# A two-block transformer kernel: activation buffers 384 bytes higher, every weight slot 192 bytes below the tokens modulo 512

## The reference

```
# first block: 16 meta tokens are put ahead of the 512
h = h + 0.5 * swiglu(rmsnorm(h, norm_ffn1), w_ffn1_in, w_ffn1_out)        # "f1" in the kernel
u = rmsnorm(h, norm_mix)
...  = split(u @ w_in)                       # forgetting attention, retention, two gates
mixed = g_a * (y_a @ w_o_fox) + g_b * (y_b @ w_o_ret)
h = h + mixed @ w_out
h = h + 0.5 * swiglu(rmsnorm(h, norm_ffn2), w_ffn2_in, w_ffn2_out)        # "f2"
# second block: 512 tokens and 256 context tokens, two layers
for l in range(2):
    y, yc = mixing_sublayer(...)             # three branches, then merge_groups(...) @ w_o
    x = layer_norm(ALPHA * x + g1 * y) * ln1_g[l] + ln1_b[l]
    x = layer_norm(ALPHA * x + g2 * swiglu_2(modulate(x, sh2, sc2), ...)) * ln2_g[l] + ln2_b[l]
    ...                                      # the context likewise, in layer 0 alone
```

## Time and profile before

| what | value |
|---|---|
| median of 3 runs | 3315.65 us (3312.38 to 3316.1) |
| profiled execution | 3318.37 us, its span 3316.6 us |
| PE busy | 3199.3 us, 96% of the span, 24458 multiplications |
| PEld busy | 2982.2 us, 90% |
| DVE, ACT, POOL busy | 1802.8, 1392.6, 482.1 us (54%, 42%, 15%) |
| mean busy share of the 16 DMA engines | 29.1% for SP's queue, 3.2% for POOL's |
| TensorE clock granted | 0.993 of full speed |

### The profile page before, as it was taken

How to read it: one execution, slowest core, us unless ns; L and a number is a source line. 1 busy time by engine, 2 the same in 40 slices (tenths; PEclk the granted TensorE clock), 3 DMA queues, 4 the chain that set the end, 5 groups by cost and what they waited for, 6 DMA issues and landing times. The chain is left out here.

```text
span 3316.6 us, 60366 instructions
## 1 busy us (share of the span) xinstructions
PE 3199.3 (96%) x24458; PEld 2982.2 (90%) x24458; DVE 1802.8 (54%) x3099; ACT 1392.6 (42%) x2533; POOL 482.1 (15%) x471
## 2 busy tenths in 40 slices
PE   8999999999999999999999999999999999989998
PEld 7999988787778899998889889999998789979997
DVE  4666553536634456666445773222227645776765
ACT  4222232337633332225447754212125557654444
POOL 1010020036500010010113201001010103111110
PEclk9999999999999999999999999999999999999999
DMA  4445422122123334453211331211214311435653
GB/s 161 165 163 175 153 75 79 59 71 65 52 77 96 108 123 170 170 175 126 68 31 35 122 115 52 64 61 61 64 58 126 101 56 46 139 88 140 165 144 99
DMA packets 107074, 339.68 MB, mean 102 GB/s; under 512 B 12144, under 2 KB 16496, under 8 KB 106672
## 3 DMA queue, kind: packets, MB, share of 16 engines
q1 hardware_dynamic: 97616, 311.65, 29.1%
q0 software_dynamic: 8752, 23.65, 3.2%
q10 hardware_dynamic: 432, 0.52, 0.0%
HBM read 324.38 MB, written 2.10 MB: 98 GB/s over the span
## 5 line engine op out<-in xcount | busy, mean ns | idle before, releaser
L2710 DVE TENSOR_TENSOR r_Wbasel<-r_Wf,r_Wbaseh 128x1024 fp32r<-128x1024 f32 (+3 forms) x286 | 359.1, 1257 | 504.3 <-ACT r_Wbaseh L2006 503.8
L2006 ACT ACTIVATE r_Wbaseh<-r_Wf 128x1024 fp32r<-128x1024 f32 (+3 forms) x286 | 291.2, 1022 | 418.3 <-PE PS L1325 313.8
L1323 PE MATMUL PS<-r_X1h,r_Wbaseh 128*128 128x264 f32 (+2 forms) x1216 | 392.2, 323 | 14.8 <-DVE r_X1l L3058 5.4
L1324 PE MATMUL PS<-r_X1l,r_Wbaseh 128*128 128x264 f32 (+2 forms) x1216 | 378.1, 311 | 0.0
L1325 PE MATMUL PS<-r_X1h,r_Wbasel 128*128 128x264 f32 (+2 forms) x1216 | 377.8, 311 | 0.0
L2710 DVE TENSOR_TENSOR r_Wtopl<-r_Wf,r_Wtoph 128x1024 fp32r<-128x1024 f32 (+3 forms) x147 | 174.1, 1185 | 207.1 <-ACT r_Wtoph L2006 206.7
L1323 PE MATMUL PS<-r_X2h,r_Wbaseh 128*128 128x256 f32 (+1 forms) x888 | 274.4, 309 | 5.8 <-DVE r_Wbasel L2710 2.5
L1325 PE MATMUL PS<-r_X2h,r_Wbasel 128*128 128x256 f32 (+1 forms) x888 | 266.7, 300 | 0.0
L1324 PE MATMUL PS<-r_X2l,r_Wbaseh 128*128 128x256 f32 (+1 forms) x888 | 266.5, 300 | 0.0
L1323 PEld LDWEIGHTS PS<-r_X1h,r_Wbaseh 128*128 128x128 f32 x1216 | 231.0, 190 | 38.1 <-issue 8.1
L1324 PEld LDWEIGHTS PS<-r_X1l,r_Wbaseh 128*128 128x128 f32 x1216 | 231.0, 190 | 13.7 <-issue 2.4
(11 more groups left out here) (520 smaller groups left out, 9971.4 us busy)
## 6 DMA issues: line engine op xcount, KB each, us to landing
r_Wf<-in_wmod SPq DMA_DIRECT2D x96, 512.0 KB, 3.6
r_Wf<-in_f_in SPq DMA_DIRECT2D x88, 512.0 KB, 4.4
r_Wf<-in_g_in SPq DMA_DIRECT2D x69, 512.0 KB, 3.5
r_Wf<-in_w_o SPq DMA_DIRECT2D x40, 512.0 KB, 4.4
r_Wf<-in_f_out SPq DMA_DIRECT2D x32, 448.0 KB, 4.2
r_Wf<-in_g_out SPq DMA_DIRECT2D x32, 448.0 KB, 3.4
r_SR<-in_g_in SPq DMA_DIRECT2D x38, 256.0 KB, 3.4
r_SR<-in_g_in POOLq DMA_DIRECT2D x38, 256.0 KB, 5.5
```

Source lines behind the costliest of these rows:

```text
L1323: self.e.matmul(o, wh, xh, start=first, stop=False)
L1324: self.e.matmul(o, wh, xl, start=False, stop=False)
L2006: e.activation(p.w(i, cols)[0], p.Wf[:, i % NW, 0:cols], ACT.Copy).then_inc(*p.hi.did(i))
L2710: e.tensor_tensor(l, p.Wf[:, i % NW, 0:cols], h.bitcast(F32), ALU.subtract).then_inc(*p.lo.did(i))
```

## The change

No instruction is added or removed. Two paddings move buffers, and the second feed-forward part of the first block gets token buffers of its own.

- `MB` moves from the top area to the end of the constants, and P0, the first byte of the token area, lies 256 + 128 = 384 bytes higher; all that is placed from P0 on moves along.
- The `mixed` and `latent` slots get 320 bytes of padding ahead of them, and TOP, the place of the `top` slots, is 320 lower.
- `n3` and `f2` use X5 instead of X1, and H2 takes its rows: 512 tokens instead of 528, so that 2048 bytes are the step of a feature tile. X5 lies in the bytes of X1.

```
-TOP = 188224
+TOP = 187904
...
+        self.MB, p = at("MB", [128, 2, 32], F32, p)
-        P0 = p
+        P0 = p + 128
...
-        self.H2[0], p = at("H2h", [128, 8, T1], F32R, P1)
-        self.H2[1], p = at("H2l", [128, 8, T1], F32R, p)
+        self.X5 = [None, None]
+        self.X5[0], p = at("X5h", [128, 8, TX], F32R, P0)
+        self.SQ5, _ = at("SQ5", [128, 8, TX], F32, P0)
+        self.XC5, _ = at("XC5", [128, 8, TX], F32, p)
+        self.X5[1], p = at("X5l", [128, 8, TX], F32R, p)
+        assert p <= P1
+        self.H2[0], p = at("H2h", [128, 8, TX], F32R, P1)
+        self.H2[1], p = at("H2l", [128, 8, TX], F32R, p)
...
-        p = self.weight_slots("mixed", 3, P2)
+        p = self.weight_slots("mixed", 3, P2 + 320)
...
-        self.MB, pm = at("MB", [128, 2, 32], F32, pm)
...
-        self.weight_slots("latent", 2, p)
+        self.weight_slots("latent", 2, p + 320)
...
-        n3 = add("n3", [a_, b_], lambda k, c: vec("ffn2", k), None, self.X1, 0, self.XC1, self.SQ1, self.PAm,
+        n3 = add("n3", [a_, b_], lambda k, c: vec("ffn2", k), None, self.X5, 16, self.XC5, self.SQ5, self.PAm,
...
-        f2 = Ffn("f2", self.X1, 0, [a_, b_], self.H2, self.TM2, n3, lambda m, c0: 0.5)
+        f2 = Ffn("f2", self.X5, 16, [a_, b_], self.H2, self.TM2, n3, lambda m, c0: 0.5)
```

## The result

The changed kernel takes 3292.36 us, the median of four runs (3288.65 to 3300.39), beside 3315.87 us for the kernel before (four runs, 3312.38 to 3316.1). The ratio is 0.9931, with a 95% interval from 0.9911 to 0.9952: 23.5 us faster, where 52.7 were forecast, and above the range of 3254 to 3285. The profiled execution is the fastest of the four, 3288.65 us. All lines of this program stand six higher than in the kernel before, so that the three multiplications are lines 1329 to 1331. Its trace lacks 16 records of one other line, 1838, which is why the page counts 16 multiplications fewer.

What follows compares the result with a forecast made beforehand. PE was taken as the bound, busy 3199.3 of 3316.6 us, its pace depending on operand addresses. Terms 31.9 + 15.5 + 8.5 + 1.9 - 2.1 = 55.7 us, less 3 for waits, gave a median of 3263 us; range 3254 to 3285.

Steps and rivals of the forecast that it cites:

- The argument from the earlier trace: Adjacent g0 streams of H3, same shape: 120.0 ns with `top` slots at distance 0, 113.3 with `base` at +192.
- Rival 3: No change: the poor state takes all the gain (3319 us), or addresses are not the cause (3316); chance 0.04.
- All 24 sums of that kind: `lin_tok` on X2, tokens stationary and weights moving, at -192 before the change; taken to show 113.3 ns for that distance.
- Rival 1: Distance -192 with stationary weights has two states; A, B and C run at 115.0 ns, 3284 us; chance 0.09.
- A: `top`, `latent` and `mixed` products going from distance 0 to -192: 4,764 multiplications at 6.7 ns, 31.9 us gained.
- B: X1 and H2 products in f2, from a changing distance to -192: 3,168 multiplications at 4.9 ns, 15.5 us gained.
- C: `base` products going from +192 to -192: 5,088, of which 1,923 in the poor state gain 4.4 ns each, 8.5 us.
- The exchange of weights and tokens: Inference that -192 gives 113.3 ns also with weights stationary and tokens moving, the reverse of `lin_tok` on X2.
- D: 512-wide YA and YB products with `base`, 384 at +192: 5 ns each, 1.9 us gained, at least nothing.
- E: `lin_tok` on X2 going from -192 to +192: 480 multiplications at 4.4 ns, 2.1 us lost, at best nothing.
- I took off 3 us: Allowance for PE waits growing, at H4's low part in g1 and at `top` weights, as PE gets faster.

Runs made afterwards that it cites:

- e6: Changed kernel with weight slots 16 bytes into their tiles and all slots at distance -112 modulo 256; 3342.08 us, ratio 1.0067 to the kernel before.
- e9: Distance -112 like e6, but with token tensors, not weights, moved 16 bytes into their allocations; 3286.33 us, ratio 0.991 to the kernel before.
- e1: Streams alone, not the whole kernel: 16 distances from -256 to 224 in steps of 32; -192 ended at 113.3 ns in 10 of 12 starts.
- e5: Streams alone, not the whole kernel: distances -128 to 120 in steps of 8, some starts behind distance 0; -112 ran at 113.3 ns behind all 15 starts.
- e8: Streams alone, not the whole kernel: four weight places by sixteen token places; at -112, 113.3 ns with weights at 0, 120.0 with weights at 16.
- e2: The change with stationary weights at +192 in place of -192, tokens left where they were; 3320.82 us, ratio 1.001 to the kernel before.

## Why the prediction was right in direction and wrong in size

**Right.** PE sets the time, the change works by addresses alone, and it makes the kernel faster. The argument from the earlier trace rows held: 113.3 ns stands where 120.0 stood. Rival 3's version in which addresses mean nothing is out: e6 and e9 issue the same instructions on other addresses, and lie 0.7% above and 0.9% below the kernel before. The Trainium skill ("SBUF — State Buffer", section "Who interferes with whom") has the single rule that only the port pair shared by VectorE and GpSimd causes contention. These runs do not agree with what the prediction drew from it, that the residues mean nothing, and the measurement decides.

**The step that failed** is "All 24 sums of that kind [...] settle at 113.3 [...] So I take 113.3 ns for distance -192." The sums, which are 20 (480 multiplications, 24 to a sum) and not 24, are not 20 observations. They stand behind four starts (at 1681.16, 1700.88, 2698.92 and 2710.48 us), and a state, once entered, mostly lasts to the next halt: in the changed kernel, 2 of the 539 sums that follow without a break on another differ from it. In the maps this residue ended good behind 34 of 48 starts from a halt or from other work, 0.71: 20 of 24 in e1 (-192 and +64), 6 of 12 in e5 and 8 of 12 in e8, there with weights at 0 or 32. In the changed kernel itself, 44 of the 80 sums that a halt or other work interrupts end good. Four good ones in a row then have a chance of 0.71^4 = 0.25, or less; that is an estimate, since it takes the starts as independent draws. Rival 1, to which I gave 0.09, named what the runs show: two states at -192. Its pace of 115.0 ns was above the measured mean of A, B and C, 114.25, and its 3284 us still came out low, because more came back than the 2 us that it took off.

The exchange of weights and tokens, which the prediction called its inference, is not needed to explain this. e2 leaves `lin_tok` on X2 at its old addresses, and behind the same wait for ZU, after which the kernel before was good (at 1700.88; its row is shown below), 96 multiplications take 11.31 us, 117.8 ns each:

```profile
1695.27 0.38 PE L1329 MATMUL PS<-r_Wbaseh,r_X2h 128*128 128x256 f32 x1 [2.49 <-ACT r_ZU L2568]
...
1698.19 0.28 PE L1329 MATMUL PS<-r_Wbaseh,r_X2h 128*128 128x256 f32 x1
...
1709.50 0.28 PE L1329 MATMUL PS<-r_Wbaseh,r_X2h 128*128 128x256 f32 x1
```

**The terms**, each as its count times the fall of its mean pace in the profiled run:

| term | pace before, after, ns | gain us | forecast us |
|---|---|---|---|
| A, 4,764 | 119.92, 114.03 | 28.1 | 31.9 |
| B, 3,168 | 118.09, 114.87 | 10.2 | 15.5 |
| C, 5,088 | 115.04, 114.07 | 4.9 | 8.5 |
| D, 384 of YA and YB | 233.33, 233.33 | 0 | 1.9 |
| E, 480 of lin_tok | 113.44, 116.92 | -1.7 | -2.1 |
| not seen: 528 of X2 at 512 columns | 229.39, 233.29 | -2.1 | none |
| sum | | 39.4 | 55.7 |

A, B and C have the right mechanism. Together they fall 12.7 us short, and the 2,529 multiplications in poor sums, at 4.4 ns each, are 11.1 of these. D set YA beside X2 at 512 columns, but both lay at +192, so what set them apart was not the distance, and YA's pace did not move with it. The last term was overlooked: X2 at 512 columns goes from +192 to -192 too, and e1 shows that to be the dearer one at that width.

**The waits were sized too small.** I took off 3 us. Splitting PE's time by the gaps between starts, the streams of these multiplications (gaps under 140 ns, or 260 at 512 columns) lost 40.8 us, their halts and slow gaps gained 6.7, and all else on PE 4.8. With 0.5 at the ends, the span falls by 29.8. So 11.5 us of what the streams gained came back, where the prediction took off 3. The waits account for 6.1 of it. Another 4 at most is clock: the granted clock stood near half for 51.7 us against 43.9, and half of the added 7.8 us is lost where PE would have been busy. Such stretches stand at halts or just behind them, but not every halt brings one. At the same wait for ZU, PE stood still for 2.49 us in the kernel before and for 2.44 in the changed one, by the timeline of each:

```profile
1700.88 0.39 PE L1323 MATMUL PS<-r_Wbaseh,r_X2h 128*128 128x256 f32 x1 [2.49 <-ACT r_ZU L2562]
...
1701.10:1703.90 2.80, 2.80 (x26) 2.80 (x26) 1.29 (x3) 2.34 (x7) 0.00 (x0) 1.00 0.02 6
```

```profile
1695.27 0.39 PE L1329 MATMUL PS<-r_Wbaseh,r_X2h 128*128 128x256 f32 x1 [2.44 <-ACT r_ZU L2568]
...
1695.80:1698.60 2.80, 2.80 (x16) 2.80 (x15) 1.32 (x2) 2.02 (x5) 0.00 (x0) 0.50 0.02 6
```

The second row of each is a window just behind (columns as in the earlier trace rows). Before, 26 multiplications run in 2.8 us at a granted clock of 1.00; afterwards 16 in the same time at 0.50, the lower of the two levels (1.2 in place of 2.4 GHz). The halt is as long, so its length alone doesn't explain the drop. In e9, the streams lost 46.7 us and 18.7 came back: 10.6 of waits, nearly 4 of clock, and the rest not traced.

The median of the changed kernel lies 3.7 us above its profiled run, that of the kernel before 2.5 below; so 29.7 us between the profiled runs are 23.5 between the medians.

**What stays open.** What makes the pace depend on the two addresses. What of a halt or a switch of work picks the state, and why e5's streams at distance 0 did not lead into the good state at +192 as those of the kernel before did. And the part of the given-back time that is neither a named wait nor clock.

## What to carry to other kernels

When the pace of a stream has states, count its starts and not its sums: the sums behind one start are one observation. Before buffers are moved to another address, run a stream of the same shape at that address, with each operand's own place and each width that the kernel uses, and choose a place that is good behind every start, as e9's was, over one that is good behind most. Where PE is busy for 96% of the span, expect part of what its streams gain to come back: here it was a quarter to two fifths (11.5 of 40.8 us, and 18.7 of 46.7 in e9), mostly in waits and in the clock.

## What the runs showed of the hardware that I had not expected

- The pace of a 128x256 float32 multiplication depends on the distance modulo 256, not 512, between the two operands: 113.3 to 121.3 ns behind most starts in e5, and 130.0 at -104 behind 6 of 15. Several distances, ±64 among them, have two steady states.
- It also depends on the weights' own place modulo 32: at distance -112, 113.3 ns with the weights at 0 and 120.0 with them at 16 (e8), which turned the best place into one that is slower than before (e6).
- What runs just before can pick the state: in the kernel before, +192 was good in 38 of 44 sums directly behind a stream at distance 0, and in 1 of 32 that a halt or other work interrupts.
- The best distance for 256 columns is not the best for 512: at -192 113.3 and 233.3 ns, at 0 120.0 and some 227 (e1). At 512 columns the distance does not decide alone: in the kernel before, YA and X2 both lay at +192 and ran at 233.3 and 229.4 ns.
